# Gated heads: logarithm and scans by direction, an exclusive reverse scan, an earlier wait for the diagonal scores, and PSUM halves exchanged behind the heads

## What is computed

```
la_f, la_b = log_sigmoid(r @ w_gate + b) / 16        # per direction, (head, token, key)
g    = cumsum(la)                                    # within a chunk
o[i] = sum_{j<=i} (q_i . k_j . exp(g_i - g_j)) v_j + (q_i exp(g_i)) @ state
o    = rms_norm(o_forward + flip(o_backward)) * gla_norm_w
y    = concat(o * silu(gate_b), conv part) @ w_out
```

## Time and profile before

| what | value |
|---|---|
| median of 3 runs | 2968.88 us (2966.89 to 2969.05) |
| the profiled execution's own time | 2971.7 us |
| its span | 2969.9 us |
| TensorE busy | 2835.9 us, 95% |
| VectorE busy | 1777.2 us, 60% |
| ScalarE busy | 1028.7 us, 35% |
| mean granted clock of TensorE | 0.973 |
| moved by DMA | 451 MB, 152 GB/s in the mean |

### The profile page before, as it was taken

How to read it: one execution, slowest core, us unless ns; L and a number is a source line. 1 busy time by engine, 2 the same in 40 slices (tenths; PEclk the granted TensorE clock), 3 DMA queues, 4 the chain that set the end, 5 groups by cost and what they waited for, 6 DMA issues and landing times.

```text
span 2969.9 us, 35322 instructions
## 1 busy us (share of the span) xinstructions
PE 2835.9 (95%) x12481; PEld 2228.2 (75%) x12481; DVE 1777.2 (60%) x2725; ACT 1028.7 (35%) x1609; POOL 15.5 (1%) x26
## 2 busy tenths in 40 slices
PE   6999998999999989999999999999999899999996
PEld 3468886776788866788878777786878688888884
DVE  6856674555587766644456547373877777425444
ACT  3032222334332245332233435343332542234224
POOL 0000000000000000000000000000000000000000
PEclk9999999999999989999999999999999999999998
DMA  9966552222356636465532222223666365333331
GB/s 342 342 217 214 188 165 86 72 72 71 107 188 215 229 107 213 174 204 190 188 104 86 71 92 83 87 85 117 213 216 202 116 227 192 99 99 98 123 113 72
DMA packets 227901, 451.26 MB, mean 152 GB/s; under 512 B 23848, under 2 KB 29434, under 8 KB 223148
## 3 DMA queue, kind: packets, MB, share of 16 engines
q1 hardware_dynamic: 224948, 440.80, 44.9%
q0 software_dynamic: 2304, 8.39, 0.8%
q10 hardware_dynamic: 504, 0.17, 0.0%
HBM read 422.01 MB, written 27.30 MB: 151 GB/s over the span
## 4 chain that ended last, share of the span: by engine, by line
PE 87%; DVE 4%; ACT 3%; issue 2%; DVEq 1%; DMA 1%; ACTq 1%; SPq 1%
PE ps L1241 21%; PE ps L1242 21%; PE ps L1245 21%; PE ps L1428 4%; PE ps L1252 3%; PE ps L1256 3%; PE ps L1253 3%; PE ps L1670 2%; PE ps L1217 1%; PE ps L1578 1%; PE ps L1587 1%; PE ps L1704 1%; PE ps L1701 1%; DMA arena<-in_w_ada 1%; PE ps L1692 1%
## 5 line engine op out<-in xcount | busy, mean ns | idle before, releaser
L1241 PE MATMUL ps<-op_hi,w_hi 128*128 128x512 f32 (+2 forms) x2928 | 1167.4, 399 | 26.6 <-DVE op_lo L1837 12.6
L1242 PE MATMUL ps<-op_lo,w_hi 128*128 128x512 f32 (+2 forms) x2928 | 1150.6, 393 | 0.0
L1728 DVE TENSOR_TENSOR w_lo<-w_raw,w_hi 128x512 fp32r<-128x512 f32 (+2 forms) x672 | 441.6, 662 | 620.0 <-ACT w_hi L649 344.3
L1245 PE MATMUL ps<-op_hi,w_lo 128*128 128x512 f32 (+2 forms) x2928 | 793.2, 391 | 4.4 <-DVE w_lo L1728 4.4
L1241 PEld LDWEIGHTS ps<-op_hi,w_hi 128*128 128x128 f32 (+1 forms) x2928 | 557.9, 191 | 152.2 <-issue 25.1
L1245 PEld LDWEIGHTS ps<-op_hi,w_lo 128*128 128x128 f32 (+1 forms) x2928 | 554.1, 189 | 122.3 <-DVE w_lo L1728 5.4
L1242 PEld LDWEIGHTS ps<-op_lo,w_hi 128*128 128x128 f32 (+1 forms) x2928 | 557.6, 190 | 114.7 <-issue 2.4
L649 ACT ACTIVATE w_hi<-w_raw 128x512 fp32r<-128x512 f32 (+2 forms) x416 | 243.5, 592 | 640.7 <-PE ps L1245 544.8
L1751 DVE SCALAR_TENSOR_TENSOR acc<-a_raw,vec,acc 128x512 f32<-128x512 f32 x525 | 381.4, 745 | 15.9 <-DMA a_raw<-in_w_ada 15.7
L674 ACT ACTIVATE w_hi<-w_raw 128x512 fp32r<-128x512 f32 x288 | 181.4, 632 | 589.9 <-PE ps L1245 456.6
L1252 PE MATMUL ps<-w_hi,op_hi 128*128 128x512 f32 x384 | 155.1, 404 | 3.3 <-ACT w_hi L649 3.3
(11 more groups left out here) (264 smaller groups left out, 2281.8 us busy)
## 6 DMA issues: line engine op xcount, KB each, us to landing
a_raw<-in_w_ada SPq DMA_DIRECT2D x216, 512.0 KB, 4.0
w_raw<-in_w_in_e SPq DMA_DIRECT2D x160, 512.0 KB, 4.7
w_raw<-in_w_in SPq DMA_DIRECT2D x96, 512.0 KB, 4.8
arena<-in_w_ada SPq DMA_DIRECT2D x72, 512.0 KB, 6.8
w_raw<-in_w_in_o SPq DMA_DIRECT2D x64, 512.0 KB, 4.3
w_raw<-in_w_out SPq DMA_DIRECT2D x32, 512.0 KB, 4.8
w_raw<-in_w_out_e SPq DMA_DIRECT2D x32, 512.0 KB, 5.0
w_raw<-in_w_out_o SPq DMA_DIRECT2D x32, 512.0 KB, 3.8
```

The costliest lines, as they stand in the source:

```text
L1241: mm(ps[0:m, bank + j, 0:tok], hi[:, cols], B.op_hi[:, k, 0:tok], start=first, stop=False)
L1242: mm(ps[0:m, bank + j, 0:tok], hi[:, cols], B.op_lo[:, k, 0:tok], start=False, stop=False)
L1245: last = mm(ps[0:m, bank + j, 0:tok], lo[:, j * P:j * P + m], B.op_hi[:, k, 0:tok], start=False, stop=last_t)
L1728: V.tensor_tensor(B.w_lo[:, c % RING, 0:width], B.w_raw[:, c // 2 % RAW, c % 2, 0:width], B.w_hi[:, c % RING, 0:width].bitcast(f32), ALU.s ...
```

## The change

- `plan` appends an empty group (name `beside`, i = 8, no tiles) behind the `beside` groups. All groups from `egb` on have an index higher by one and so use the other four banks: `egb` 0 now banks 0 to 3.
- ScalarE takes the logarithm in two instructions, one per direction, each with its own signal.
- VectorE forms the gates of direction 0, signals `logits_read`, scans G, forms the gates of direction 1, makes the low tile that stood ahead of the scans, and scans E.
- The E scan is exclusive at once: it starts one column later, adds the gate of the column before and multiplies by the restart mask. Its first column is cleared by a memset. The subtraction is gone; the block totals of E are now E's last column plus the last gate.
- The diagonal scores wait for `logits_read` instead of `totals`.
- The product of the diagonal scores with the identity stands behind the first level's weighting; the wait for the diagonal scores stays where it was.
- `egb` 0 waits for `beside_left` (banks 0 to 3 copied out) and `egb` 1 for `heads_done`; the wait at the end of `gla_tensor` is gone.

```diff
--- before.py
+++ after.py
@@ -55,6 +55,7 @@
     add("eq", E_IN, 2080, 2, "T", 3)
     add("ev", E_IN, 1024, 2, "N", 3)
     add("beside", E_IN, 4128, 2 * GLA_HEADS, "T", 3)
+    g.append(dict(g[-1], i=2 * GLA_HEADS, kt=0))
     add("egb", E_IN, 3104, 2, "T", 3)
     add("wo2", "w_out_e_2", 0, 4, "T", 4)
     add("xp", "w_in_o_2", 0, 4, "T", 5)
@@ -1154,7 +1155,8 @@
         Act(tmp, tmp, ACT.Exp, scale=-1.0)
         high_to(6)
         nc.scalar.drain()
-        Act(tmp, tmp, ACT.Ln, bias=1.0).then_inc(sem("g_log"), 1)
+        for d in range(2):
+            Act(tmp[:, 2 * d:2 * d + 2, :], tmp[:, 2 * d:2 * d + 2, :], ACT.Ln, bias=1.0).then_inc(sem("g_log"), 1)
         high_to(9)
 
         act.wait_ge(sem("totals"), i + 1)
@@ -1197,7 +1199,7 @@
         Act(at(AT_R, 1, S), at(AT_R, 1, S), ACT.Exp, scale=-0.5).then_inc(sem("o_deviation"), 1)
         high_to(36)
 
-    nc.scalar.drain().then_inc(B.bank_free[(FIRST["egb"] - 1) % 2], GLA_HEADS)
+    nc.scalar.drain().then_inc(B.bank_free[(FIRST["egb"] - 1) % 2], GLA_HEADS + 1)
     nc.scalar.drain().then_inc(B.bank_free[FIRST["egb"] % 2], GLA_HEADS)
 
 
@@ -1260,9 +1262,15 @@
 
         g = GROUPS[n]
         c = lambda v, per: v if r is None else r * per + v
-        if n >= 2:
+        if n == FIRST["egb"]:
+
+            pe.wait_ge(sem("beside_left"), 4 + 8 * GLA_HEADS)
+        elif n >= 2:
 
             pe.wait_ge(B.bank_free[n % 2], c(n // 2, 1))
+        if n == FIRST["egb"] + 1:
+
+            pe.wait_ge(sem("heads_done"), GLA_HEADS + 1)
         pending = n >= 2 and GROUPS[n - 2]["part"] is not None
         taken = c(ordinal(n - 1), 2) if pending else None
         hook = n >= 1 and GROUPS[n - 1]["part"] is not None
@@ -1650,7 +1658,7 @@
         last.then_inc(sem("g_logits"), 1)
         tiles(T_LOGIT)
 
-        pe.wait_ge(sem("totals"), i + 1)
+        pe.wait_ge(sem("logits_read"), i + 1)
         pe.wait_ge(sem("head_staged"), i + 1)
         for b in range(NT):
             for a in range(2):
@@ -1709,7 +1717,6 @@
         for a in range(2):
             last = mm(ps[:, 6, :], B.ones, tmp[:, a, :], start=a == 0, stop=a == 1)
         last.then_inc(sem("o_summed"), 1)
-    pe.wait_ge(sem("heads_done"), GLA_HEADS + 1)
 
 
 
@@ -2409,24 +2416,30 @@
         low_to(5)
         kh, qh = Y[:, bass.ds(i * 2, 2), :], Y[:, bass.ds(i * 2 + 8, 2), :]
 
-        dve.wait_ge(sem("g_log"), i + 1)
-        V.scalar_tensor_tensor(out=tmp, in0=ps[:, 4:8, :], scalar=0.0, in1=tmp, op0=ALU.min, op1=ALU.subtract)
-        low_to(6)
+        V.memset(E[:, :, 0:1], 0.0)
+
+        dve.wait_ge(sem("g_log"), i * 2 + 1)
+        V.scalar_tensor_tensor(out=tmp[:, 0:2, :], in0=ps[:, 4:6, :], scalar=0.0, in1=tmp[:, 0:2, :],
+                               op0=ALU.min, op1=ALU.subtract).then_inc(sem("logits_read"), 1)
         V.drain()
         for a in range(2):
             V.tensor_tensor_scan(G[:, a, :], B.restart, tmp[:, a, :], 0.0, ALU.mult, ALU.add)
-            V.tensor_tensor_scan(E[:, a, :], B.restart, tmp[:, 2 + a, :], 0.0, ALU.mult, ALU.add)
+        dve.wait_ge(sem("g_log"), i * 2 + 2)
+        V.scalar_tensor_tensor(out=tmp[:, 2:4, :], in0=ps[:, 6:8, :], scalar=0.0, in1=tmp[:, 2:4, :],
+                               op0=ALU.min, op1=ALU.subtract)
+        low_to(6)
+        V.drain()
+
+        for a in range(2):
+            V.tensor_tensor_scan(E[:, a, 1:S], tmp[:, 2 + a, 0:S - 1], B.restart[:, 1:S], 0.0, ALU.add, ALU.mult)
         V.drain()
         V.tensor_copy(tot[:, 0:8].unsqueeze(2), t8(G)[:, :, P - 1:P])
-        V.tensor_copy(tot[:, 8:16].unsqueeze(2), t8(E)[:, :, P - 1:P]).then_inc(sem("totals"), 1)
+        V.tensor_tensor(tot[:, 8:16].unsqueeze(2), t8(E)[:, :, P - 1:P], t8(tmp[:, 2:4, :])[:, :, P - 1:P],
+                        ALU.add).then_inc(sem("totals"), 1)
         V.drain()
         low_to(9)
 
-        V.tensor_tensor(E, E, tmp[:, 2:4, :], ALU.subtract)
         dve.wait_ge(sem("diagonal"), i + 1)
-        V.tensor_tensor(am_diag, ps[:, 4, :].rearrange("p (b t) -> p b t", t=P),
-                        B.eye2.unsqueeze(1).to_broadcast([P, NT, P]), ALU.mult)
-        V.drain()
 
         sums = at(AT_G, 2, 2, S)
         both = Y.rearrange("p (w t) s -> p w t s", w=2)[:, :, bass.ds(i * 2, 2), :]
@@ -2467,6 +2480,10 @@
             dve.wait_ge(sem("decays"), i * len(LEVELS) + n + 1)
             m = level_buffer(B, n)
             V.tensor_tensor(m, m, both, ALU.mult).then_inc(sem("weighted"), 1)
+            if n == 0:
+                V.tensor_tensor(am_diag, ps[:, 4, :].rearrange("p (b t) -> p b t", t=P),
+                                B.eye2.unsqueeze(1).to_broadcast([P, NT, P]), ALU.mult)
+                V.drain()
             if n >= 1:
                 take(n - 1)
                 if n + 1 < len(LEVELS):

```

More of the change, by code:

```diff
@@ L2410, in gla_vector @@
         kh, qh = Y[:, bass.ds(i * 2, 2), :], Y[:, bass.ds(i * 2 + 8, 2), :]
-        dve.wait_ge(sem("g_log"), i + 1)
-        V.scalar_tensor_tensor(out=tmp, in0=ps[:, 4:8, :], scalar=0.0, in1=tmp, op0=ALU.min, op1=ALU.subtract)
+        V.memset(E[:, :, 0:1], 0.0)
[4 more added lines that the diff above has]
+        for a in range(2):
+            V.tensor_tensor_scan(G[:, a, :], B.restart, tmp[:, a, :], 0.0, ALU.mult, ALU.add)
+        dve.wait_ge(sem("g_log"), i * 2 + 2)
+        V.scalar_tensor_tensor(out=tmp[:, 2:4, :], in0=ps[:, 6:8, :], scalar=0.0, in1=tmp[:, 2:4, :],
+                               op0=ALU.min, op1=ALU.subtract)
         low_to(6)
@@ L2416, in gla_vector @@
         for a in range(2):
-            V.tensor_tensor_scan(G[:, a, :], B.restart, tmp[:, a, :], 0.0, ALU.mult, ALU.add)
-            V.tensor_tensor_scan(E[:, a, :], B.restart, tmp[:, 2 + a, :], 0.0, ALU.mult, ALU.add)
+            V.tensor_tensor_scan(E[:, a, 1:S], tmp[:, 2 + a, 0:S - 1], B.restart[:, 1:S], 0.0, ALU.add, ALU.mult)
         V.drain()
         V.tensor_copy(tot[:, 0:8].unsqueeze(2), t8(G)[:, :, P - 1:P])
-        V.tensor_copy(tot[:, 8:16].unsqueeze(2), t8(E)[:, :, P - 1:P]).then_inc(sem("totals"), 1)
+        V.tensor_tensor(tot[:, 8:16].unsqueeze(2), t8(E)[:, :, P - 1:P], t8(tmp[:, 2:4, :])[:, :, P - 1:P],
+                        ALU.add).then_inc(sem("totals"), 1)
         V.drain()
         low_to(9)
-        V.tensor_tensor(E, E, tmp[:, 2:4, :], ALU.subtract)
         dve.wait_ge(sem("diagonal"), i + 1)
-        V.tensor_tensor(am_diag, ps[:, 4, :].rearrange("p (b t) -> p b t", t=P),
-                        B.eye2.unsqueeze(1).to_broadcast([P, NT, P]), ALU.mult)
-        V.drain()
         sums = at(AT_G, 2, 2, S)
```

## The result

The changed kernel's median is 2948.02 us (6 runs, 2941.47 to 2954.59), that of the kernel before in the same session 2967.89 us: ratio 0.9937, 95% interval 0.9923 to 0.9952, so 19 us faster, with 2949.6 us forecast. Run once more on another occasion, it had 2952.66 against 2966.53: ratio 0.9948 (0.9932 to 0.9964).

What follows compares the result with a forecast made beforehand. TensorE, busy 95% of the span, was taken as the bound, leaving its idle and half-clocked time to win. 12.1 (heads) + 5.4 + 1.8 (behind them) = 19.3 us, giving 2952.4 profiled, 2949.6 as a median; range 2945 to 2957.

Steps and rivals of the forecast that it cites:

- Heads, 12.1 to 12.4 us: Four heads, Ln to level 0: 2.5 us gained in head 1, 3.3 in the others; 12.4 in all, 12.1 taken.
- the 2.5 of the chain: VectorE from Ln to the first weighting's end: done at + 18.25 instead of + 20.75, 2.5 us a head.
- Behind the heads, 5.4 + 1.8 us: At egb's start, the exchange of banks saves 5.4 us of idle time and 1.8 us of half clock.
- the load that I watched: SyncE's load of egb's tiles 8 and 9: not moved, needed 7 us earlier, with 13.5 us left for it.
- The wait at tile 5: TensorE in each head: new wait of 1.0 to 1.5 us for tile 5's low part, about 0.2 in head 1.
- The halves and the fixed cost: Split logarithm and gates: start 0.86 us earlier, 0.07 more for gates; by the skill's fixed term 0.16 more a head.
- The reversed scan: E scans with add before multiply: taken as equal in cost; bounds from -1.1 to +2.3 us per head.
- Rival 3: Reversed scan twice as slow: E's scans take 2.3 us more a head, gain 10.1, 2958.8 us; chance 0.04.
- Rival 1: Short gaps at tile 5 and level 0 still let the clock fall: gain 15.1, 2953.8 us; chance 0.08.
- Rival 2: Exchange of banks brings nothing, early egb tiles meeting late weights or low parts: gain 12.1, 2956.8 us; chance 0.05.
- rival 4: Slower: the wait at tile 5 starts a long half-clocked run over the diagonal scores, about 2988 us; chance 0.03.
- Margins: TensorE ready 0.9 us ahead of VectorE at level 0; some 2.4 us remain between second weighting and level 1's scores.

Runs made afterwards that it cites:

- experiment 7: The changed kernel with the diagonal scores waiting for the totals again as well: ratio 0.9963 to the kernel before.
- experiment 3: The kernel before with only the diagonal scores' wait changed, from the totals to the gates' reading of the logits: ratio 1.0002 over 12 runs.
- experiment 1: The kernel before with the exchange of banks alone (empty group and the waits of egb), heads untouched: ratio 0.9965.
- experiment 5: The changed kernel with the low tile of index 5 back ahead of the scans of G: ratio 0.9931 to the kernel before.
- experiment 9: The changed kernel with one logarithm and one gate operation over both directions again: ratio 0.9952 to the kernel before.

## Why the prediction was right

- **Heads, 12.1 to 12.4 us: 12.3** at level 0 against the profile that the forecast was read from. Each step of VectorE's chain came out: Ln to gates 1.10 (1.09 forecast), E's scans begin at + 6.57 (6.6), low tiles at + 9.48 (9.5), first distance at + 11.29 (11.3), weighted at + 18.26 (18.25). Single edits undone one at a time cost 0.79 (halves), 1.13 without the extra drain (subtraction) and 0.77 (mask product) a head; less 0.17 for the added drain (the scans of G start 1.31 us behind gates that take a step of 1.14) this is the 2.5 of the chain. The earlier wait has 1.1 a head beside them (experiment 7); alone it gave 2.3 us at level 0 and no time (experiment 3). That the number fits so closely is partly luck: the term counts 0.8 us in three heads for a fall of the clock that comes in some executions only, and with experiment 1's profile as the start it would have been 10.8. At the last level it is 11.6, or 10.3.
- **Behind the heads, 5.4 + 1.8 us: 5.4 and 1.65**, and the same alone (experiment 1). That the shift is kept to the end was assumed in the forecast; the tails of the profiles bear it out within their scatter of 3 us. The low part of tile 2 was ready about 1 us before it was needed, without a wait; the load that I watched was issued 10.0 us after TensorE's restart (2037.88), where 4.6 us stood before, and nobody waited for it.
- **The wait at tile 5 was mis-sized:** 1.3, 2.6, 1.0 and 1.3 us instead of 0.2 to 1.5. Its end was right (+ 6.5), its start is where TensorE is, and that depends on how long the clock is low at the gate logits. In head 2 there was no such stretch; in head 2 of the second profile it was 6.8 us long, and 0.2 us of wait at tile 5 was left. It cost nothing (experiment 5), but at 3.4 us it would have (experiment 9).
- **The halves and the fixed cost.** Experiment 9 measured 0.79 us a head for the halves, the figure from the rows. By the fixed term of about 150 cycles of the Trainium skill (VectorE: DVE Perf Modes, the section on the TRN2 errata) they would be worth 0.7, an estimate, with the term charged once, as in the prediction, or 0.54 with it charged for both extra instructions, as in experiment 9's expectation. The trace agrees with the term in the durations (0.68, 1.22 and 2.29 us for 512, 1024 and 2048 elements leave 0.15 beside the elements) and not in the starts, which are 0.60, 1.13 and 2.21 us apart and leave 0.07: where no drain lies between, about half of the fixed part lies over the neighbour's work.
- **The reversed scan** takes 2.34 us for two over 511 elements, the other order 2.34 for two over 512: no difference. Rival 3 falls. (Its bound of 2.4 us each is a doubled duration, its 2.3 us a head a doubled spacing; it doesn't matter here.) The Trainium skill (DVE: opcode table, instruction layouts, handler registers and perf-mode slots, section 6) says that a scan runs at half throughput and puts that on the way back to an earlier stage. The trace agrees with the rate, two scans of 512 elements starting 1.13 us apart where two plain operations start 0.60 apart; no run here shows its cause.
- **Rival 1** didn't come in either profile of the changed kernel, nor behind any single gap as short as it named. Its price was about right: in experiment 9 a fall behind a gap of 3.40 us made level 0 0.84 us later, beside 0.6 us of waiting that it used up, so 3.4 us at half clock cost some 1.45 us and not 1.7. Rival 2 showed nowhere. Nearest to rival 4 came head 3 of experiment 7: two gaps, 6.8 us at half clock over the diagonal scores, 2.8 us lost.
- **Margins.** TensorE waited 0.6 us for the first weighting, 0.9 were forecast. The second weighting ended at 1671.63 + 2.29 = 1673.92, 2.5 us ahead of level 1's scores (2.4 forecast).

## What to carry to other kernels

A wait in the list is worth only what the next chain leaves: before removing it, add up the other engine's work to the next meeting point. Here 12.9 us of waits were worth nothing until VectorE's chain was shortened, and level 0 1.4 us earlier was worth nothing until the tiles behind it, and the places where they are made, were changed too. Compare intervals between named instructions; they repeat to 0.05 us where spans scatter by ten.

## What was unexpected of the hardware

- A gap of a few microseconds makes TensorE's clock fall in some cases only. Over all profiles here, 12 gaps of 3.1 to 3.8 us in the heads were followed by a half-clocked stretch 7 times; the gaps of 5.9 us behind the heads 3 times of 3; a single gap of up to 2.6 us at tile 5, the diagonal scores or the first level never. Two gaps of 2.6 and 1.6 us, one tile part apart, did it once.
- The clock also falls for 3.4 or 6.8 us at the gate logits (L1649: few rows, float32), with a gap of 0.4 us or none ahead of them, in 46 of the 56 heads of the 14 profiles. Half-clocked time goes with the scatter of 10 us between executions of one kernel: among 18 runs of the kernel before in one session, from 2963 to 2975 us, the mean granted clock goes from 0.976 to 0.972 (correlation -0.80). How much of it lies in the heads differs: of the 23.9 us more at half clock in the second profile of the changed kernel, 17.1 lie ahead of them.
